# Stage borders of a two-block network: half-row sums of squares, fused scale and residual, another order of the last down-projection pairs, and GpSimd's residual between its weight sums

## What is computed

```python
# first block, layer i
h = _layer_norm(DN_ALPHA * h + mixer(h), ln1_g[i], ln1_b[i])
u = jnp.square(jax.nn.relu(h @ mlp_w1[i])) @ mlp_w2[i]          # 1024 -> 4096 -> 1024
h = _layer_norm(DN_ALPHA * h + u, ln2_g[i], ln2_b[i])
h = h + jax.nn.sigmoid(h @ ple_gate_w[i]) * (p[i] @ ple_w[i])
# second block, layer l
x = x + 0.5 * rms_norm(swiglu(rms_norm(x, ffn1_pre_g[l]), ...), ffn1_post_g[l])   # 1024 -> 2816 -> 1024
x = x + rms_norm(hybrid_mix(rms_norm(x, mix_pre_g[l]), ...), mix_post_g[l])
x = x + 0.5 * rms_norm(swiglu(rms_norm(x, ffn2_pre_g[l]), ...), ffn2_post_g[l])
```

## Time and profile before

| | us |
|---|---|
| median of 3 runs | 2066.53 |
| lowest, highest | 2061.09, 2070.67 |
| the profiled execution, as timed | 2056.4 |
| its span, first to last instruction | 2054.6 |
| PE busy in it | 2004.0 (98%) |

### The profile page before, as it was taken

One profiled execution on the slowest core, in us unless ns is written; L12 is line 12 of the kernel. 1 busy time (PEld: TensorE's weight loads), 2 busy tenths in 40 slices (PEclk: granted clock), 3 DMA queues, 4 the chain that ended last, 5 costly groups with the idle time before them and its releaser, 6 DMA issues.

```text
span 2054.6 us, 31876 instructions
## 1 busy us (share of the span) xinstructions
PE 2004.0 (98%) x12016; PEld 1549.2 (75%) x12016; DVE 1088.1 (53%) x1959; ACT 345.4 (17%) x772; POOL 636.9 (31%) x665
## 2 busy tenths in 40 slices
PE   8999999999999999999999999999999999999998
PEld 6875995468769944699658869994899478869973
DVE  4343866434638655346636544665456636444564
ACT  1332000012420000300024511000200025310000
POOL 0000644310106453134412603434234405312342
PEclk9999999999999999999999989999999999989999
DMA  8422544443144444354435116544744344025453
GB/s 312 142 68 73 191 174 168 147 152 128 56 146 172 164 179 159 120 203 170 164 133 164 53 34 199 174 148 143 268 172 175 145 155 143 11 93 185 166 180 117
DMA packets 82935, 305.46 MB, mean 149 GB/s; under 512 B 9264, under 2 KB 9392, under 8 KB 82416
## 3 DMA queue, kind: packets, MB, share of 16 engines
q1 hardware_dynamic: 80496, 294.93, 40.9%
q0 software_dynamic: 2304, 8.65, 1.2%
HBM read 302.23 MB, written 1.05 MB: 148 GB/s over the span
## 4 chain that ended last, share of the span: by engine, by line
PE 92%; DVE 4%; ACT 1%; DVEq 1%; issue 1%; DMA 0%; POOL 0%; ACTq 0%; SPq 0%
PE psum L439 26%; PE psum L478 21%; PE psum L242 9%; PE psum L867 8%; PE psum L1814 6%; PE psum L2363 4%; PE psum L315 4%; PE psum L302 3%; PE psum L454 3%; PE psum L326 3%; PE psum L1673 1%; PE psum L451 1%; PE psum L283 1%; PE psum L2738 1%; PE psum L1751 0%
## 5 line engine op out<-in xcount | busy, mean ns | idle before, releaser
L439 PE MATMUL psum<-sq,space 128*128 128x128 f32 x2400 | 302.7, 276 | 0.0
L439 PEld LDWEIGHTS psum<-sq,space 128*128 128x128 f32 x2400 | 286.2, 193 | 0.0
L478 PE MATMUL psum<-space,cat 128*128 128x512 f32 x456 | 208.2, 592 | 0.0
L242 PE MATMUL psum<-h,ring 128*128 128x256 f32 x864 | 195.4, 386 | 7.0 <-DMA ring<-in_weights 7.0
L242 PEld LDWEIGHTS psum<-h,ring 128*128 128x128 f32 x864 | 166.7, 194 | 32.6 <-issue 9.7
L478 PEld LDWEIGHTS psum<-space,cat 128*128 128x128 f32 x456 | 86.4, 189 | 109.3 <-issue 109.3
L405 POOL TENSOR_TENSOR space<-ring 128x512 f32<-128x512 f32 x50 | 66.3, 1326 | 316.7 <-PE psum L439 265.4
L478 PE MATMUL psum<-ring,space 128*128 128x512 f32 x304 | 144.2, 594 | 6.8 <-DVE space L424 6.8
L664 POOL TENSOR_TENSOR cat<-space 128x128 f32<-128x128 f32 x76 | 59.6, 784 | 213.3 <-PE psum L478 213.3
L439 PE MATMUL psum<-sq,ring 128*128 128x128 f32 x800 | 107.7, 278 | 9.1 <-DVE space L410 9.1
L478 PEld LDWEIGHTS psum<-ring,space 128*128 128x128 f32 x304 | 56.7, 189 | 78.7 <-issue 66.4
(11 more groups left out here) (411 smaller groups left out, 3302.8 us busy)
## 6 DMA issues: line engine op xcount, KB each, us to landing
ring<-in_weights SPq DMA_DIRECT2D x552, 512.0 KB, 4.1
space<-in_rows POOLq DMA_DIRECT2D x8, 512.0 KB, 8.5
space<-in_gains POOLq DMA_DIRECT2D x6, 512.0 KB, 4.3
const<-in_consts SPq DMA_DIRECT2D x1, 1493.0 KB, 11.0
h<-in_x SPq DMA_DIRECT2D x1, 1024.0 KB, 4.8
x<-in_x_tok SPq DMA_DIRECT2D x1, 1024.0 KB, 15.3
out<-x SPq DMA_DIRECT2D x2, 512.0 KB, 2.6
space<-in_params POOLq DMA_DIRECT2D x2, 509.5 KB, 7.0
```

Source lines behind the costliest of these rows:

```text
L242: last = pe.matmul(out, unit[:, i, :], rhs[:, i, :], start=(i == 0), stop=(i == KD - 1), skip_group_check=True)
L439: last = pe.matmul(out, weights(i), tokens(i), start=(i == 0), stop=(i == 3), skip_group_check=True)
L478: return pe.matmul(k.psum[:, bank, :], lhs, rhs, start=(p == 0), stop=(p == fn.downs - 1), skip_group_check=True)
```

## The change

1. `act_boundary`, `dve_boundary`: the sum of squares of a row is made in two halves of 512 columns, the first as soon as those columns are there (`y_half`, `x_half`); the first half's sum becomes the bias of the root of the second. The multiplication by the gain is done on each half before the root is known, and one instruction a half then scales by the reciprocal and adds the residual (`scalar_tensor_tensor` of `scaled`, `r` and `x`). The joined parts go to SBUF (`s.y`) and not back to PSUM.
2. `pe_ffn`: the last four pairs run in the order 1, 2, 3, 6, 5, 7, 4; the wait for VectorE's and GpSimd's sums stands ahead of part 3 and no longer ahead of part 1.
3. `pe_lead` has a new wait for `y_half` halfway through its units in three of the borders (the sum that reads bank 6 now stands behind the scaling into `tmp`).
4. `tail_pool`, `pool_ffn`: GpSimd waits for VectorE's first weight sums, makes the sums of job 1, then the residual of tokens 0, the sums of job 3, the residual of tokens 1, and then loads the rows of LN2. In the second block too GpSimd's first sums now wait for VectorE's first sums. One of the FFN's buffers (`pre`) moves out of `tmp`, which is still read then.
5. `tail_vector`: LN2 is done by halves too (`upper_rows`, `lower_rows`): the residual is added to the parts as they come, and the statistics of a half are taken at once.

```diff
@@ pe_lead @@
         for out in outs[len(units):last]:
+            if freed is not None and len(units) == len(outs) // 2:
+                pe.wait_ge(*freed)
@@ pe_ffn @@
     last_pairs = range(fn.downs - TAIL, fn.downs)
+    pe.wait_ge(k.hid_ready, fn.hid0 + fn.tiles)
     for p in last_pairs:
-        take(p)
+        units[p] = pe_take(k, pe, w), pe_take(k, pe, w)
         last = part(1, p)
+    last.then_inc(k.part_done, 1)
+    for p in last_pairs:
+        last = part(2, p)
+    last.then_inc(k.part_done, 1)
+    for p in last_pairs:
+        pe.wait_ge(*fn.summed(k, fn.jobs + p))
+        pe.wait_ge(k.hid_summed, fn.down0 + p + 1)
+        last = part(3, p)
...
@@ pool_ffn @@
-    pool.wait_ge(k.y_done, 2 * n_in + 2)
+    pool.wait_ge(k.dve_summed, fn.dve0 + 1)
     for i in range(1, fn.jobs, 2):
         in_sums(k, b, pool, fn, i, k.pool_summed)
+        if between is not None and i < 4:
+            between(i // 2)
@@ act_boundary @@
+            act.wait_ge(k.y_half, 2 * (ffn.n - 2) + tt + 1)
+            act_half_square(k, s, act, tt, s.y[:, tt * 512:tt * 512 + 512], scale, eps)
+            act.wait_ge(k.y_done, 2 * g + tt + 1)
+            act_root_of_sum(k, s, act, tt, s.y[:, (1 - tt) * 512:(1 - tt) * 512 + 512], scale).then_inc(s.y_std, 1)
...
+def act_half_square(k, s, act, tt, src, scale, eps, done=None):
+    first = act.activation(s.squares[:, 0:512], src, ACT.Square, accum_out=s.stat[:, tt:tt + 1])
...
+    act.drain()
+    act.activation(s.stat[:, 6 + tt:7 + tt], s.stat[:, tt:tt + 1], ACT.Identity, bias=k.eps(eps), scale=scale / D)
+def act_root_of_sum(k, s, act, tt, src, scale):
+    act.activation(s.squares[:, 512:1024], src, ACT.Square, accum_out=s.stat[:, 8 + tt:9 + tt])
+    act.drain()
+    return act.activation(s.stat[:, 2 + tt:3 + tt], s.stat[:, 8 + tt:9 + tt], ACT.Sqrt, bias=s.stat[:, 6 + tt:7 + tt],
+                          scale=scale / D)
@@ dve_boundary @@
-        dve.scalar_tensor_tensor(s.scaled, k.acc_tok[:, tt, :], r, s.gain, ALU.mult, ALU.mult)
...
-        dve.tensor_tensor(k.x_tok[:, tt, :], k.x_tok[:, tt, :], s.scaled, ALU.add).then_inc(s.x_new, 1)
+        for b, done in ((tt, s.x_half), (1 - tt, s.x_new)):
+            cols = slice(b * 512, b * 512 + 512)
+            dve.scalar_tensor_tensor(k.x_tok[:, tt, cols], s.scaled[:, cols], r, k.x_tok[:, tt, cols], ALU.mult,
+                                     ALU.add).then_inc(done, 1)
@@ tail_vector @@
+    def lower_rows(y, parts):
+        left, right = y[:, 0:512], y[:, 512:1024]
+        dve.wait_ge(k.part_done, 6 * fn.n + 6)
+        dve.tensor_tensor(k.upper, k.shared, k.psum[:, 3, :], ALU.add)
+        dve.drain()
+        plus_residual(right, right, k.upper)
+        dve.tensor_tensor(right, right, k.psum[:, 6, :], ALU.add).then_inc(k.parts_free, 1)
+        plus_residual(left, left, k.upper)
+        dve.bn_stats(parts[:, 1, :], right)
```

More of the change, by code:

```diff
@@ L291, in pe_normed, with pe_lead @@
     pe.wait_ge(k.h_high, 2 * n + tt + 1)
-def pe_lead(k, pe, w, outs, n, early, src, done):
+def pe_lead(k, pe, w, outs, n, early, src, done, freed=None):
     units = []
@@ L507, in pe_ffn @@
             last = part(name, p)
+            if name == 6 and p == last_pairs[0]:
+                last.then_inc(k.freed, 2)
         last.then_inc(k.part_done, 1)
     for p in last_pairs:
[L510 to L517 removed]
         last = part(7, p)
[L519 to L520 removed]
     last.then_inc(k.part_done, 1)
@@ L535, in act_ffn @@
             k.act_ready, 1)
-    if before_pairs is not None:
-        before_pairs()
     for q in range(fn.pairs):
@@ new lines, in act_root_of_sum, with act_first_turned @@
+def act_root_of_sum(k, s, act, tt, src, scale):
[3 more added lines that the diff above has]
+                          scale=scale / D)
+def act_first_turned(k, s, act, g, tt, gain):
+    act.wait_ge(k.h_turned, (2 * g + tt) * 2 + 1)
+    for j in range(4):
+        last = act.activation(k.h[:, j, half(tt)], k.bank(2 * tt, P)[:, j, :], ACT.Identity, scale=s.p(gain, j))
+    last.then_inc(k.h_low, 1)
@@ L699, in act_rms_gained, with gained, half_sum, last_sum @@
                    scale=1.0 / D).then_inc(s.x_std, 1)
-    act.wait_ge(k.h_turned, (2 * g + tt) * 2 + 1)
-    for j in range(4):
-        last = act.activation(k.h[:, j, half(tt)], k.bank(2 * tt, P)[:, j, :], ACT.Identity, scale=s.p(gain, j))
-    last.then_inc(k.h_low, 1)
+    act_first_turned(k, s, act, g, tt, gain)
 def dve_boundary(k, s, dve, n, gain, meanwhile=None, ffn=None):
     g = border(1, 0, n)
+    def gained(b, src):
+        cols = slice(b * 512, b * 512 + 512)
+        return dve.tensor_tensor(s.scaled[:, cols], src, s.gain[:, cols], ALU.mult)
+    def half_sum(b, left, op, right, done):
+        out = s.y[:, b * 512:b * 512 + 512]
+        dve.tensor_tensor(out, left, right, op).then_inc(done, 1)
+        dve.drain()
+        gained(b, out)
+    def last_sum():
+        dve.drain()
+        dve.tensor_tensor(s.y[:, 512:1024], k.upper, k.psum[:, 6, :], ALU.add).then_inc(k.y_half, 1)
     dve.wait_ge(s.gain_loaded, 16 * (n + 1))
     for tt in range(2):
-        if ffn is not None:
-            (dve_join_last if tt else dve_join_first)(k, dve, ffn)
+        if ffn is None:
+            dve.wait_ge(k.y_done, 2 * g + tt + 1)
+            gained(1 - tt, k.psum[:, 1 + tt, :]).then_inc(s.y_gained, 1)
+            dve.wait_ge(s.y_squared, 2 * (n // 3) + tt + 1)
+            gained(tt, k.psum[:, 3 * tt, :])
+        elif tt == 0:
+            dve.wait_ge(k.part_copied, ffn.n + 1)
+            dve.wait_ge(k.part_done, 6 * ffn.n + 2)
+            half_sum(0, k.copied, ALU.add, k.psum[:, 0, :], k.y_half)
+            dve_join_parts(k, dve, ffn)
+            dve.wait_ge(k.part_done, 6 * ffn.n + 5)
+            half_sum(1, k.lower, ALU.add, k.psum[:, 6, :], k.y_done)
+        else:
+            dve.drain()
+            gained(1, s.y[:, 512:1024])
+            dve.wait_ge(k.job_done, ffn.job0 + ffn.jobs + ffn.downs)
+            half_sum(0, k.upper, ALU.subtract, k.psum[:, 2, :], k.y_done)
+        if tt == 0 and meanwhile is not None:
+            meanwhile()
         r = s.stat[:, 4 + tt:5 + tt]
@@ L2767, in tail_scalar @@
     norm(LN1, "ln1_g", "ln1_b")
-    act_ffn(k, f, act, Ffn(layer), lambda: act.wait_ge(f.residual, 2 * (2 * layer) + 2))
+    act_ffn(k, f, act, Ffn(layer))
     norm(LN2, "ln2_g", "ln2_b")
@@ L2814, in norm @@
             if which == LN2 and tt == 0:
-                dve_join_middle(k, dve, Ffn(layer))
+                lower_rows(k.x_tok[:, 1, :], f.ln_parts[:, 2:4, :])
             dve.wait_ge(k.h_turned, (2 * n + tt) * 2 + 2)
@@ L2822, in tail_vector @@
     norm(LN1, "ln1_g", "ln1_b")
-    dve_ffn(k, f, dve, Ffn(layer), border(0, layer, LN1), lambda: dve.wait_ge(f.residual, 2 * (2 * layer) + 2))
+    dve_ffn(k, f, dve, Ffn(layer), border(0, layer, LN1))
     norm(LN2, "ln2_g", "ln2_b")
```

188 lines of the change are left out of this document (105 added, 83 removed).

## The result

The changed kernel took 2032.61 us (median of 4 runs, 2031.98 to 2036.47), the kernel before beside it 2067.99 us (2061.09 to 2070.67). The ratio is 0.984, with an interval of 0.981 to 0.987. The forecast of 2037.0 was 4.4 us too high. The gain, measured side by side, was 35.4 us between the medians (1.6%, interval 28 to 39 us), where 29.4 had been summed.

What follows compares the result with a forecast made beforehand. PE was taken to bound the kernel, busy for 2004.0 of 2054.6 us. Gains of 6.8 + 14.1 + 6.8 + 1.7 = 29.4 us off the median of 2066.5 gave 2037.1 us (2027.0 against the profiled execution), range 2022 to 2053.

Steps and rivals of the forecast that it cites:

- The sum: Whole kernel: gains of 6.8, 14.1, 6.8 and 1.7 us, 29.4 in all, taken off the median of 2066.5 us.
- Last pairs, 6.8: Last down pairs: PE's six waits for VectorE's sums go, as the wait moves back by eight products; 6.8 us.
- Start of the first block's FFNs, 14.1: With GpSimd held back, PE's waits for VectorE's weight sums go, 9.1 us, and 5.0 us of low clock with them.
- the spare time at jobs 3 and 5: First block's FFNs: GpSimd's sums, now behind its residuals, are done 4 to 5 us before PE asks; cost nothing.
- the collision moves: Rival: GpSimd's sums of job 3 or 5 come late, two stalls of 2 to 5 us, 2044 us; chance 9%.
- Borders, 6.8: Second block's borders: shorter chains cut stalls before the transposes, 4.6 us for tokens 0 and 2.2 for tokens 1.
- End, 1.7: End of the kernel: the last norm, run with PE stopped, gets shorter by 0.42 and 1.25 us; 1.7 us.
- LN2, 0: First block's LN2: PE has no stall there, so nothing is won; fused instructions held by GpSimd's residual all just fit.
- Clock, 5.0: Low clock behind the stalls at the start of the first block's FFNs goes with them, 2.3 + 2.7 = 5.0 us.

Runs made afterwards that it cites:

- wait_only: The kernel before, parts in their old order, with only the last four pairs' wait for the sums moved from part 1 to part 6: 2055.8 us, ratio 0.998.
- rows_by_scalar: The changed kernel with LN2's gain and bias rows loaded from ScalarE's queue and no longer from GpSimd's: 2029.2 us, ratio 0.984.
- fill: The kernel before with 16 idle products on PE ahead of job 0's wait in the first block's two FFNs: 2059.6 us, ratio 0.9995.
- before_again: The kernel before, unchanged, run and traced a second time: 2060.0 us, ratio 0.9998.
- border_back: The changed kernel with the second block's borders as before (whole-row squares, scaling and residual apart): 2041.4 us, ratio 0.989.
- pool_back: The changed kernel with GpSimd's LN1 residual back ahead of all its sums, without the wait for VectorE's first sums in the first block: 2039.9 us, ratio 0.988.
- pool_behind: The changed kernel with GpSimd's LN1 residual behind VectorE's first sums but ahead of all GpSimd's own sums: 2045.7 us, ratio 0.991.
- best: The changed kernel with LN2's rows loaded from ScalarE's queue and the gain's multiplication of tokens 1's second half on GpSimd: 2027.4 us, ratio 0.985.

## Why the prediction was right, and where it was off

**The sum.** Summed were 29.4 us; 22.5 + 5.7, that is 28.3 us, came against the usual time of before. By this count the base was off. I took the gain off a median of three runs, although the profiled execution lay 10 us lower and nothing said why. All runs of before say: the three were high. 2061.4 - 29.4 would have been 2032.0, against the 2032.6 measured. This reading isn't shown to the end. Against the runs beside it the changed kernel won 35.4 us, 6 more than summed, and whatever made those runs of before longer may have left the changed kernel alone; that their idle time was the usual one is likely (the groups of before differ in low clock and not in span x clock), but their clocks aren't on record. That the forecast of the time came within 4.4 us owes something to luck, since the median of before alone moved by 8 us.

**Last pairs, 6.8.** As summed. The new order moves the wait by eight products; that it was needed was not right: four are enough (`wait_only`), in the old order of the parts.

**Start of the first block's FFNs, 14.1.** The mechanism is as told. VectorE's four sums, behind which GpSimd now waits, in the timeline after:

```profile
217.81 0.69 DVE L408 TENSOR_TENSOR space<-ring 128x512 f32<-128x512 f32 x1
...
219.94 0.69 DVE L413 TENSOR_TENSOR space<-ring,space 128x512 f32<-128x512 f32 x1
...
224.13 1.06 PE L443 MATMUL psum<-sq,ring 128*128 128x128 f32 x8
```

They end at 220.6, 3.5 us before PE asks at 224.1: the 3.5 of the sum. (The whole stretch lies 2.7 us later in this trace than in that of before, so 218 in the prediction is 220.6 here.) Clock, in the same two stretches as the earlier trace rows:

```profile
226.00:231.00 5.00, 5.00 (x47) 5.00 (x46) 4.80 (x4) 0.28 (x1) 4.86 (x3) 1.00 0.75 246
627.00:633.00 6.00, 6.00 (x56) 6.00 (x55) 5.78 (x8) 0.28 (x1) 5.86 (x4) 1.00 0.59 195
```

The step that failed here is the spare time at jobs 3 and 5. Job 3 had it. For job 5 the "4 to 5 us to spare" turned into waits of 0.17 us (first layer) and 0.88 us (second). Counted from the end of VectorE's first sums, the estimate had GpSimd's sums of job 5 done after 30 us and PE asking after 34; they were done after 35.0, and PE asked after 34.9. Of the 5.0 us, 4.47 are the time in which GpSimd did nothing behind the two issues, for which the estimate had no term at all; all else together was 0.6 us long. `rows_by_scalar` shows that this time goes when another engine issues the DMAs. So PE did wait at job 5, as the rival "the collision moves" had it, but for another cause and 1.0 us in place of its 7.

**Borders, 6.8.** The traced stalls fell by 8.45 - 1.48 = 7.0 us. Chain of tokens 0, ScalarE and VectorE after:

```profile
1044.05 0.63 ACT L704 ACTIVATE sq<-space 128x512 f32<-128x512 f32 x1 [9.12 <-DVE space L737]
...
1045.42 1.42 DVE L771 SCALAR_TENSOR_TENSOR x<-sq,space,x 128x512 f32<-128x512 f32 x2
...
1049.14 1.03 PE L284 MATMUL psum<-const,tmp 128*128 128x128 f32 x8
```

From VectorE's last join (1043.33) to the transposes, ahead of which PE now shows no idle time, it is 5.8 us, against 7.4: 1.6 shorter, where 1.65 was summed. The square of 512 columns took 0.63 (taken: 0.60), a fused half 0.71 to 0.76 (0.65). Tokens 1 keep 0.74 us of stall, where 0.8 was forecast:

```profile
1057.34 1.09 PE L284 MATMUL psum<-const,tmp 128*128 128x128 f32 x8 [0.74 <-DVE tmp L790]
```

**End, 1.7.** 7.91 us after PE's last product became 6.36: 1.6. The last norm's two fused halves are one row:

```profile
2030.15 1.41 DVE L771 SCALAR_TENSOR_TENSOR x<-sq,space,x 128x512 f32<-128x512 f32 x2
```

**LN2, 0.** The two fused instructions of `lower_rows` ran beside GpSimd's residual and were held, the third, earlier one wasn't:

```profile
397.88 0.69 DVE L2854 SCALAR_TENSOR_TENSOR x<-x,rstd 128x512 f32<-128x512 f32 x1
...
403.99 2.20 DVE L2854 SCALAR_TENSOR_TENSOR x<-x,hid_act 128x512 f32<-128x512 f32 x1
...
407.22 1.74 DVE L2854 SCALAR_TENSOR_TENSOR x<-x,hid_act 128x512 f32<-128x512 f32 x1
...
403.30 2.34 POOL L2954 TENSOR_TENSOR x<-tmp,space 128x1024 f32<-128x1024 f32 x1 [17.08 <-DVE tmp L2911]
405.78 2.62 POOL L2956 TENSOR_TENSOR x<-x,space 128x1024 f32<-128x1024 f32 x1
```

Counted from VectorE's join at 399.79, the first ends at 6.4, the banks are free at 7.5, the scaled tokens 1 at 14.5 with PE's transposes at 14.5 without a gap: the forecast's 6.4, 7.2 and 14.3. By the rule of the Trainium skill (SBUF — State Buffer, Who interferes with whom) that was to be expected, and the trace agrees: 2.20 and 1.74 us against 0.69. It decided nothing here, but little was to spare, as the figures say.

**Clock, 5.0.** 5.7 us between the means of before and after. `fill` shows the cause at the FFNs, 4.6 us on average. `wait_only` and `before_again` show low stretches behind the stalls ahead of the transposes too, which the sum had left out; the trace that the prediction read happened to have none of them. What these cost on average isn't shown. Two runs speak against a simple sum: `border_back` and `pool_back` bring the stalls back and have the low clock of the changed kernel, 32.1 and 31.6 us. With four runs each they can't rule out the 5 us, but they don't bear it out.

## What to carry to other kernels

A wait can be cured by moving it a few products back on the engine that waits; the order of the work need not change for it. Where two engines hold each other up, a long instruction goes where both still have time before their next deadline, not just behind the other engine's first one: `pool_behind` lost 13 us to the changed kernel with the same work and the same first wait. Before a forecast is tied to a median of three, ask for more runs of the base, or give the range the distance to the profiled execution. A kernel that is run at another time than its rival is compared through the base that ran beside each: medians alone put `best` 5 us ahead, and the ratios put it level.

## What the runs showed of the hardware that was not expected

GpSimd stood for 4.47 us in the middle of its vector work, at the first `drain` behind two DMA issues of its own (1.12 us for both), and not when ScalarE's queue issued them. It did so in every trace with these issues there, for 2.2 to 5.6 us. What it does in that time no row shows.

Stalls of 1.9 to 2.1 us were followed by PE's lower clock level at some times (0.66 and 0.72 over 5 to 6 us) and by the full clock at others, in `fill` within one execution.

ScalarE's square with a running sum took 0.63 us for 512 columns and 1.02 to 1.06 for 1024, and its 1-column instruction 0.29. So some 0.2 us of a square don't depend on its length, and halving it saved 0.4.
